# Expert layers: gate and up products in fp32, or as three products of operands split on chip

## What is computed

```python
expert_id = g_idx * EXPERTS_PER_GROUP + e_idx          # 2 of 32 experts for each token
hid = silu(einsum('td,edf->tef', xt, w_gate)) * einsum('td,edf->tef', xt, w_up)
y = einsum('tef,efd->td', hid * cw[:, :, None], w_down)
```

## Time and profile before

| What | Value |
|---|---|
| Median of 3 runs | 1228.33 us (1228.23 to 1233.76) |
| The profiled execution: its own time | 1233.52 us |
| Its span in the trace | 1231.7 us |
| Granted TensorE clock, mean | 0.95 |
| PE, DVE, ACT busy | 1123.2, 601.6, 537.0 us |
| Matmul instructions | 5580 |
| Bytes moved by DMA | 210.68 MB |

### The profile page before, as it was taken

How to read it: one execution, slowest core, us unless ns; L and a number is a source line. 1 busy time by engine, 2 the same in 40 slices (tenths; PEclk the granted TensorE clock), 3 DMA queues, 4 the chain that set the end, 5 groups by cost and what they waited for, 6 DMA issues and landing times.

```text
span 1231.7 us, 15828 instructions
## 1 busy us (share of the span) xinstructions
PE 1123.2 (91%) x5580; PEld 911.6 (74%) x5580; DVE 601.6 (49%) x1177; ACT 537.0 (44%) x1020; POOL 72.1 (6%) x111
## 2 busy tenths in 40 slices
PE   5958889999998997899899999978979899999977
PEld 4857677999997885797677777756867687777756
DVE  4536675666666564555523223256645532232344
ACT  4435564444444532584433332245566443322234
POOL 8000600000000020000100000000000100000000
PEclk8988699999999998999999999979989999999989
DMA  9683013666654543003658888513501948888700
GB/s 293 174 216 133 1 35 120 205 189 186 188 169 166 168 152 137 1 2 137 256 202 297 303 304 286 178 53 119 170 1 38 353 142 300 297 307 290 237 0 35
DMA packets 105075, 210.68 MB, mean 171 GB/s; under 512 B 7992, under 2 KB 49816, under 8 KB 104752
## 3 DMA queue, kind: packets, MB, share of 16 engines
q1 hardware_dynamic: 101984, 204.04, 48.7%
q0 software_dynamic: 2736, 4.80, 2.1%
q10 hardware_dynamic: 288, 0.99, 0.2%
HBM read 207.17 MB, written 2.62 MB: 170 GB/s over the span
## 4 chain that ended last, share of the span: by engine, by line
PE 83%; DVE 7%; ACT 5%; issue 3%; DMA 2%; SPq 1%; ACTq 0%; DVEq 0%
PE bank L787 21%; PE bank L1448 20%; PE bank L1465 10%; PE bank L1179 8%; PE bank L1189 7%; PE bank L882 3%; PE bank L706 2%; PE bank L863 2%; PE bank L1490 2%; PE bank L871 2%; PE bank L1907 1%; ACT x_high L760 1%; DMA ring<-in_w_uq 1%; PE bank L1335 1%; PE bank L862 1%
## 5 line engine op out<-in xcount | busy, mean ns | idle before, releaser
L787 PE MATMUL bank<-weight_parts,x_high 128*128 128x512 f32 (+3 forms) x832 | 248.8, 384 | 27.3 <-issue 13.8
L1448 PE MATMUL bank<-expert_w,block_x 128*128 128x256 f32 x1120 | 260.6, 379 | 1.0 <-ACT block_x L1414 1.0
L1448 PEld LDWEIGHTS bank<-expert_w,block_x 128*128 128x128 f32 x1120 | 207.3, 190 | 59.9 <-issue 33.0
L787 PEld LDWEIGHTS bank<-weight_parts,x_high 128*128 128x128 f32 x832 | 157.1, 196 | 58.3 <-issue 20.3
L808 DVE TENSOR_TENSOR weight_parts<-ring,weight_parts 128x1024 fp32r<-128x1024 f32 (+3 forms) x108 | 121.2, 1141 | 91.4 <-ACT weight_parts L805 91.2
L787 PE MATMUL bank<-weight_parts,x_low 128*128 128x512 f32 (+3 forms) x416 | 158.8, 382 | 0.0
L805 ACT CAST weight_parts<-ring 128x1024 fp32r<-128x1024 f32 (+3 forms) x108 | 103.8, 982 | 118.6 <-PE bank L787 91.5
L1465 PE MATMUL bank<-expert_w,junk 128*128 128x512 f32 x280 | 131.7, 593 | 0.8 <-issue 0.8
L1516 DVE SCALAR_TENSOR_TENSOR arena<-bank,home_w,arena 128x1024 f32 x64 | 82.2, 1284 | 79.4 <-PE bank L1465 79.4
L1503 DVE TENSOR_TENSOR junk<-junk,bank 128x128 f32<-128x128 f32 x70 | 20.2, 288 | 176.0 <-ACT junk L1427 176.0
L1179 PE MATMUL bank<-x_high,parts 128*128 128x256 f32 x512 | 98.5, 285 | 0.6 <-DVE parts L1243 0.6
(11 more groups left out here) (320 smaller groups left out, 1430.5 us busy)
## 6 DMA issues: line engine op xcount, KB each, us to landing
expert_w<-in_moe_w_gate SPq DMA_DIRECT2D x70, 512.0 KB, 5.2
expert_w<-in_moe_w_up SPq DMA_DIRECT2D x70, 512.0 KB, 6.1
expert_w<-in_moe_w_down SPq DMA_DIRECT2D x70, 512.0 KB, 4.2
ring<-in_w_ff SPq DMA_DIRECT2D x64, 512.0 KB, 3.9
ring<-in_w_in SPq DMA_DIRECT2D x16, 512.0 KB, 11.1
ring<-in_a_w_in SPq DMA_DIRECT2D x16, 512.0 KB, 4.6
ring<-in_ple_w_gate SPq DMA_DIRECT2D x16, 512.0 KB, 5.0
ring<-in_w_o SPq DMA_DIRECT2D x8, 512.0 KB, 6.4
```

What stands on the lines that cost most here:

```text
L787: mm = nc.tensor.matmul(bank[:, j["m"] % 4, 0:n], j["operand"][x][:, 2 * c + kk, at[0]:at[1]], weight_parts[:, number % PAIRS, w, kk * n:( ...
L1448: mm = nc.tensor.matmul(bank[:, 4 + b % 2, 0:256].rearrange("p (q n) -> p q n", q=2), block_x[:, b % 2, k, :], w[:, k], start=k == 0, stop ...
```

## The change

For gate and up the expert layers go over to three products of split operands; the down product stays in fp32.

- The weights of a block (2048 columns of gate and up) are rounded by ScalarE into `expert_high` (two buffers; new function `act_cast_expert`) and VectorE subtracts that from the weights, in place (`dve_split_expert`). For blocks 0 and 1 this is done in two halves of 1024 columns and ahead of time, for the others in one instruction.
- The sorted input is kept as `sorted_high` (ScalarE, as before) and `sorted_low` (VectorE, new `dve_sort`). Each block copies both: high by ScalarE (1024 columns), low halved between ScalarE (512) and VectorE (512).
- TensorE runs `gate_up` in one piece of 24 products, then `turn_hid(b-1)`, then `low(b-2)`, one block later than before. `add` on VectorE lags by three blocks.
- The tile registers are loaded for eight blocks at a time.
- `DEPTH` goes from 7 to 5, since `expert_high` needs space. `ple_y` and `place_turned` move to other places in SBUF.
- The second half of `dve_route` (the shares of the tokens, `cw`, and the masks) becomes `dve_masks` and is called in `dve_experts` after the sort, the first copies and the split of block 1. `pe_shares` still waits for `cw`. `pe_gather` waits for `sorted_split` of a chunk where it waited for `sorted_ready`.
- In `pe_combine` tile 0 is multiplied in fp32 straight from `acc`; tiles 1 to 3 are split as before.

```diff
-BLOCKS, DEPTH = EXPERTS + EXTRA, 7
+BLOCKS, DEPTH = EXPERTS + EXTRA, 5
...
     def pe_gather(pe, layer):
...
-                    pe.wait_ge(sorted_ready, KB * layer + k - 3)
+                    pe.wait_ge(sorted_split, KB * layer + k - 3)
...
+    def dve_sort(dve, layer):
+        for k in range(KB):
+            dve.wait_ge(sorted_ready, KB * layer + k + 1)
+            nc.vector.scalar_tensor_tensor(out=sorted_low[:, k, :], in0=bank[:, 4 + k % 4, :],
+                                           scalar=gains[f"ln_ffn{layer}"][:, k:k + 1], in1=sorted_high[:, k, :],
+                                           op0=ALU.mult, op1=ALU.subtract).then_inc(sorted_split, 1)
...
+    def act_cast_expert(act, layer, b):
+        act.wait_ge(*up_at(layer, b))
+        if b >= 2:
+            act.wait_ge(ex_up, BLOCKS * layer + b - 1)
+        if b >= 2:
+            nc.scalar.copy(expert_high[:, b % 2, :], expert_w[:, b % DEPTH, 0:2048]).then_inc(ex_cast, 2)
+            return
+        for j in range(2):
+            nc.scalar.copy(half_of(expert_high[:, b % 2, :], j),
+                           half_of(expert_w[:, b % DEPTH, 0:2048], j)).then_inc(ex_cast, 1)
+    def dve_split_expert(dve, layer, b, halves=(0, 1)):
+        if b >= 2:
+            dve.wait_ge(ex_cast, 2 * (BLOCKS * layer + b) + 2)
+            nc.vector.tensor_tensor(expert_low[:, b % DEPTH, 0:2048], expert_w[:, b % DEPTH, 0:2048],
+                                    expert_high[:, b % 2, :], ALU.subtract).then_inc(ex_split, 2)
+            return
...
     def act_experts(act, layer):
...
+        def copy_x(b):
+            if b < EXPERTS and b % 8 == 0:
+                tiles.extend(tiles_of(act, b))
+            at = tiles[b] * P if b < EXPERTS else (b - EXPERTS + 1) * P
+            nc.scalar.copy(block_high[:, b % 2], sorted_high[:, :, ds(at, P)]).then_inc(ex_copied, 1)
+            nc.scalar.copy(block_low[:, b % 2, 4:8], sorted_low[:, 4:8, ds(at, P)]).then_inc(ex_copied, 1)
...
         for b in range(BLOCKS):
             act.wait_ge(ex_up, first + b + 1)
             nc.scalar.activation(silus[:, b % 2, :], bank[:, 4 + b % 2, 0:P], ACT.Silu).then_inc(ex_silu, 1)
+            if b:
+                keep(b - 1)
             if b + 2 < BLOCKS:
-                act_block_x(act, layer, b + 2)
-            act.wait_ge(ex_turned, first + b + 1)
-            nc.scalar.copy(hidTs[:, b % 2, :], bank[:, 6 + b % 2, 0:P]).then_inc(ex_kept, 1)
+                act_cast_expert(act, layer, b + 2)
+                copy_x(b + 2)
...
     def pe_experts(pe, layer):
...
+            for k in range(KB):
+                if k % 4 == 0:
+                    pe.wait_ge(ex_split, 2 * (first + b) + k // 4 + 1)
+                for n, (x, w) in enumerate(((block_high, high), (block_high, low), (block_low, high))):
+                    mm = nc.tensor.matmul(bank[:, 4 + b % 2, 0:256].rearrange("p (q n) -> p q n", q=2),
+                                          x[:, b % 2, k, :], w[:, k], start=k == 0 and n == 0,
+                                          stop=k == KB - 1 and n == 2)
...
+        for b in range(BLOCKS + 2):
+            if b < BLOCKS:
+                gate_up(b)
+            if 1 <= b <= BLOCKS:
                 turn_hid(b - 1)
...
+            if b >= 2:
+                low(b - 2)
...
     def pe_combine(pe, layer):
+        pe.wait_ge(ex_added, BLOCKS * (layer + 1))
+        for t in range(TILES):
+            for half in range(2):
+                nc.tensor.matmul(bank[:, 2 * t + half, :], place_turned[:, 0, t * P:(t + 1) * P].bitcast(F32),
+                                 acc[:, half * 512:(half + 1) * 512], start=True, stop=False)
+        for q in range(1, SORT_TILES):
...
     def dve_experts(dve, layer):
...
+        dve.wait_ge(sorted_split, KB * (layer + 1))
+        copy_x(0)
+        copy_x(1)
+        dve_split_expert(dve, layer, 1)
+        dve_masks(dve, layer)
         dve.wait_ge(acc_zeroed, layer + 1)
         for b in range(BLOCKS):
             hid(b)
-            if b:
-                add(b - 1)
-        add(BLOCKS - 1)
+            if b + 2 < BLOCKS:
+                copy_x(b + 2)
+            if b >= 3:
+                add(b - 3)
+            if b + 2 < BLOCKS:
+                dve_split_expert(dve, layer, b + 2)
+        for b in range(BLOCKS - 3, BLOCKS):
+            add(b)
...
     def dve_route(dve, layer):
...
         dve.wait_ge(chosen_made, layer + 1)
+        dve_split_expert(dve, layer, 0, (0,))
...
         v.tensor_copy(steps_i[:, EXPERTS:EXPERTS + EXTRA], strays[:, :]).then_inc(steps_ready, 1)
+        dve_split_expert(dve, layer, 0, (1,))
+        dve_sort(dve, layer)
...
     def pe_moe_and_ple(pe, layer):
...
-        pe.wait_ge(sorted_ready, KB * (layer + 1))
...
     def act_moe_and_ple(act, layer):
...
         act_split_rows(act, layer)
+        act_cast_expert(act, layer, 0)
         act_embed(act, layer)
         act_route(act, layer)
+        act_cast_expert(act, layer, 1)
         act_sort(act, layer)
```

More of the change, by code:

```diff
@@ L1403, in act_sort @@
             act.wait_ge(gathered, KB * layer + k + 1)
-            nc.scalar.activation(sorted_x[:, k, :], bank[:, 4 + k % 4, :], ACT.Copy,
+            nc.scalar.activation(sorted_high[:, k, :], bank[:, 4 + k % 4, :], ACT.Copy,
                                  scale=gains[f"ln_ffn{layer}"][:, k:k + 1]).then_inc(sorted_ready, 1)
[L1406 to L1414, removed]
+    def dve_sort(dve, layer):
[4 more added lines that the diff above has]
+                                           op0=ALU.mult, op1=ALU.subtract).then_inc(sorted_split, 1)
@@ new lines, in dve_split_expert @@
+    def dve_split_expert(dve, layer, b, halves=(0, 1)):
[4 more added lines that the diff above has]
+            return
+        for j in halves:
+            dve.wait_ge(ex_cast, 2 * (BLOCKS * layer + b) + j + 1)
+            nc.vector.tensor_tensor(half_of(expert_low[:, b % DEPTH, 0:2048], j),
+                                    half_of(expert_w[:, b % DEPTH, 0:2048], j),
+                                    half_of(expert_high[:, b % 2, :], j), ALU.subtract).then_inc(ex_split, 1)
@@ L1416, in act_experts, with tiles_of @@
+    def tiles_of(eng, b):
+        _, tiles = nc.values_load_multi_w_load_instructions(steps_i[0:1, b:b + 8], engines=[eng.engine], min_val=0,
+                                                            max_val=SORT_TILES - 1)
+        return tiles
     def act_experts(act, layer):
@@ L1418, in act_experts @@
         act.wait_ge(steps_ready, layer + 1)
-        act_block_x(act, layer, 0)
-        act_block_x(act, layer, 1)
+        tiles = []
+        def copy_x(b):
[4 more added lines that the diff above has]
+            nc.scalar.copy(block_low[:, b % 2, 4:8], sorted_low[:, 4:8, ds(at, P)]).then_inc(ex_copied, 1)
+        act.wait_ge(sorted_ready, KB * (layer + 1))
+        act.wait_ge(sorted_split, KB * (layer + 1))
+        copy_x(0)
+        copy_x(1)
         act.wait_ge(place_flipped, layer + 1)
@@ L1424, in act_experts, with keep @@
                            bank[:, half, :]).then_inc(place_kept, 1)
+        def keep(b):
+            act.wait_ge(ex_turned, first + b + 1)
+            nc.scalar.copy(hidTs[:, b % 2, :], bank[:, 6 + b % 2, 0:P]).then_inc(ex_kept, 1)
         for b in range(BLOCKS):
@@ L1438, in pe_experts, with gate_up @@
         first = BLOCKS * layer
[L1440 to L1451, removed]
+        def gate_up(b):
+            pe.wait_ge(ex_copied, 2 * (first + b) + 2)
+            pe.wait_ge(ex_copied_low, first + b + 1)
+            if b >= 2:
+                pe.wait_ge(ex_hid, first + b - 1)
+            high, low = (w.rearrange("p (q k n) -> p k q n", q=2, k=KB)
+                         for w in (expert_high[:, b % 2, :], expert_low[:, b % DEPTH, 0:2048]))
+            for k in range(KB):
[5 more added lines that the diff above has]
+                                          stop=k == KB - 1 and n == 2)
+            mm.then_inc(ex_up, 1)
         def turn_hid(b):
@@ L1490, in pe_combine @@
                         mm = nc.tensor.matmul(bank[:, 2 * t + half, :], place_turned[:, q, t * P:(t + 1) * P],
-                                              x[:, q, half * 512:(half + 1) * 512], start=q == 0 and x is acc_high,
+                                              x[:, q, half * 512:(half + 1) * 512], start=False,
                                               stop=q == SORT_TILES - 1 and x is acc_low)
@@ L1517, in add, with copy_x @@
                                    scalar=share_of, in1=here, op0=ALU.mult, op1=ALU.add).then_inc(ex_added, 1)
+        tiles = []
+        def copy_x(b):
+            if b < EXPERTS and b % 8 == 0:
+                tiles.extend(tiles_of(dve, b))
+            at = tiles[b] * P if b < EXPERTS else (b - EXPERTS + 1) * P
+            if b >= 2:
+                dve.wait_ge(ex_up, first + b - 1)
+            v.tensor_copy(block_low[:, b % 2, 0:4], sorted_low[:, 0:4, ds(at, P)]).then_inc(ex_copied_low, 1)
```

(5 more changed lines are left out.)

105 lines of the change are left out of this document (60 added, 45 removed).

## The result

| | before | after |
|---|---|---|
| median of the runs, us | 1233.31 (1227.09 to 1236.37, 14 runs) | 1222.95 (1219.32 to 1225.92, 14 runs) |
| ratio, after to before | | 0.9922, 95% interval 0.9903 to 0.994 |
| span of the profiled execution, us | 1231.7 | 1220.5 |
| granted clock, mean | 0.950 | 0.945 |

The change made the kernel 10.4 us (0.8%) faster; 23.6 were forecast. It went the way that was forecast and has 0.44 of the size. The predicted 1204.7 us is 18.3 us too low; 5 us of that are the base (1228.33 in the runs shown then, 1233.31 in those beside the changed kernel), 13.2 are the change. 1222.95 lies 0.95 us above the range of 1194 to 1222.

What follows compares the result with a forecast made beforehand. TensorE was taken to bound the kernel. Per layer, -20.7 (blocks) + 13.5 (start) - 0.85 (last low) - 3.8 (combine) = -11.8 us; two layers, -23.6 from 1228.3, give 1204.7 us, range 1194 to 1222.

Steps and rivals of the forecast that it cites:

- TensorE's part: Expert blocks: 24 fp32r products in 2.87 us replace 3.46 us of fp32; block 4.70 us, 20.7 us less a layer.
- ScalarE and VectorE in a block: Each block: ScalarE needs 4.1 to 4.5 us and VectorE 4.31, with registers 4.3 to 4.9, against TensorE's 4.70.
- the price of the tile registers: Loading eight tile registers at once: 0.4 us at a layer's start, between 0 and 0.35 us in a block.
- The order of the start: Layer start: `cw` reaches TensorE 9.1 us later, half clock adds 2.7; with 1.7 of bubble, +13.5 us.
- The bubble at gate_up(2): Layer start: TensorE waits 1.7 us for the cast and split of block 2.
- The last down product: End of a layer: idle time of 0.85 us ahead of the last low goes, -0.85 us.
- The combine: End of a layer: tile 0 needs only the add, 10.2 us against 14.1, -3.8 us.
- Weights: Up weights land at 7.6 us, the cast wants them at 8.3, TensorE stalls only past 9.9; cost nothing.
- the rival's mechanism: Slower than before through late weights: `act_cast_expert` waits for gate and up, blocks of 5.73 us, 1277 us; chance 5%.
- The splitters set the pace: VectorE needs 4.8 to 5.0 us a block, each block loses 0.1 to 0.3: 1212 to 1226 us; chance 18%.
- no net change: Gains at both ends of a layer fail and VectorE needs 5.0 us a block: 1222 to 1234 us; chance 4%.

Runs made afterwards that it cites:

- two runs with 16 products: Changed kernel without the third gate/up product (low input times high weights): 1192.26 us; the same with gate and up weights issued before the down wait: 1175.24 us.
- both edits: Changed kernel with tile registers loaded singly and `cw` made between sort chunks 3 and 4: 1198.7 us, ratio 0.9732 to the kernel before.
- combine split: Changed kernel with the combine back to four split tiles, tile 0 included: 1227.11 us, ratio 0.9962 to the kernel before.

## Why the forecast came out too large

- **TensorE's part: right.** 24 products in 2.87 us, blocks of 4.70. The 0.120 of the row held against the 0.109 of the Trainium skill's formula ("TensorE: Matmul & The Clock Gate", Back-to-back issue gap).
- **ScalarE and VectorE in a block: right in the durations**, on the safe side in the sum (VectorE 3.93 where 4.31 was reckoned). Neither adds time where no registers are loaded.
- **The failed step is the price of the tile registers**: "then registers 0.4" at the start, and "eight at once ..., so between 0 and 0.35" in a block. I spread the 0.35 of a single load over a group, or took the group for one of them. It is 2.9 to 3.3 us in a row on VectorE, up to 2.8 on ScalarE. Spread over eight blocks that is 0.4 each, below the slack; but it arrives at once, ahead of all that the engine has still to do, and TensorE pays 1.0 to 1.4 of it each time. Before showed 0.35 per single load; times eight that is 2.8. Behind the groups the blocks lose 3.4 us in layer 0 and 3.0 in layer 1. At the start the group takes 2.9 us more than its term of 0.4 in layer 0 and 2.6 more in layer 1; the other steps there came out 1.1 us quicker than reckoned, so that the first gate_up is 1.8 and 1.5 us later than forecast. That makes 9.7 in two layers; the run with single registers gives 8.2 us back, out of a miss of 13.2.
- **The order of the start: right in kind.** `cw` is what holds TensorE, the shares and flips run at half clock behind it (5.03 us; forecast 5.5), and moving `cw` is worth 13.5 us for two layers. The size is 1.8 us short in layer 0 and 1.5 in layer 1, the registers again.
- **The bubble at gate_up(2): right**, 1.65 us against 1.7. What had no term is the clock of the first two gate_up, 0.5 us in layer 0 and 1.1 in layer 1: the half clock was reckoned to end with the flips.
- **The last down product: mis-read.** The term of -0.85 came out as -0.36. The chain of before shows 0.40 idle us ahead of the last low (802.66 to 803.06), not 0.85; the rest was a difference of rounded sums and a last product that is recorded 0.25 longer and still is.
- **The combine: right**, -3.4 against -3.8, and the clock stayed up through its wait of 1.38 us.
- **Weights: right at this pace**, issue to landing 7.2 in place of 6.1; with the 1.5 of the queue's position 8.7 us, past the 8.3 at which the cast wants it and below the 9.9 where TensorE stalls. The two runs with 16 products show that the rival's mechanism exists and sets in just below this pace; at this pace it shows as single stalls, 0.65 us in the changed kernel.
- **The rivals.** "The splitters set the pace" named the right engine and the wrong reason: it gives 1212 to 1226 and the result is in there, but its loss was to be spread over every block; the traces show it in three places a layer. 1222.95 also lies inside the 1222 to 1234 of "no net change", whose conditions did not come true: the gain at the end of a layer is there and VectorE needs 3.93, not 5.0. That the result falls into either range is luck.
- **The miss as a whole.** By the ledgers the two layers gain 14.2 us less than forecast: 9.7 (registers), 1.6 (clock of the first gate_up), 1.0 (last down product), 0.8 (combine), 0.65 (late up load) and 0.4 (bubble). Outside them 1.7 us were gained that were not forecast, so that the traces miss 12.4 and the medians 13.2. The runs isolate the first alone, at 8.2; the others are read from the traces and were not tried by themselves.

## What to carry to other kernels

Price a group of register loads as one stall of n times the single load, at the place where it stands in its engine's order, not as an average over what it serves: 0.77 us of slack in each of eight blocks did not hide 3 us that came once in eight blocks. When work is put ahead of others on an engine, look for small results queued behind it (here seven instructions on 128x64 values, worth 13.5 us) and who waits for them. When a ring of buffers gets shallower, put the loads that are wanted first ahead of the wait for the slot that comes free last; here it cost nothing that the runs resolve at 4.70 us a block and gave 17 us at two products. When a wait in front of a stretch is cut, look whether TensorE's half clock is gone with it or has moved to the next wait.

## What the runs showed of the hardware that was not expected

- Loading tile registers: on VectorE 0.60 us for the load of a group (0.85 the first time) and 0.28 for each value, on ScalarE 0.55 (0.76 the first time) and about 0.22.
- VectorE's instructions in a row overlap by about 0.08 us each as recorded: 4.26 us of durations in 3.93. A sum of mean durations overstates what it needs by 8%.
- TensorE's clock: after 1.00, 1.38 and 1.65 idle us the next products ran at full clock (2.4 GHz); after 3.87 us 24 products took 5.5 us at 1.2 GHz. In between the fall can come late: after 2.00 idle us (both edits) 0.8 us of products ran at full clock and then 3.7 us at 0.54; after 3.71 (combine split) three products at full clock and then 3.4 us at 0.43 us each, where full clock gives 0.23.
- The up load's time from issue to landing rose from 6.1 us at 291 GB/s to 7.2 at up to 328 GB/s.
